# A three-block fp32 network on one core: the softmax weights in one VectorE pass, the convolution's taps earlier, and the order of work around them

## What is computed

```python
mx = silu_c @ w_ada[i] + b_ada[i]              # shifts and scales, 6 x 1024 per stream
hx = modulate(rmsnorm(x, norm1_g[i]), sx1, ax1)
px = hx @ w_in[i]                              # conv input (2 x 512), q, k, v, gates
...
z = a * sigmoid(g)                             # then 31-tap depthwise conv over tokens,
...                                            # LayerNorm over 512 channels, silu
q_x = apply_rope(rmsnorm(q_x, q_norm_g[i]), cos, sin)   # rms per head part of 64
...
p = jax.nn.softmax(s, axis=-1)                 # two maps per head
w = p[:, :, 0] - lam * p[:, :, 1]
out = einsum('bhqk,bkhv->bqhv', w, vals)       # per head RMSNorm after it
```

## Time and profile before

| | |
|---|---|
| median of 3 runs | 2174.09 us |
| profiled execution, its own time | 2172.95 us |
| its span in the profile | 2171.2 us |
| TensorE matmul busy | 2041.7 us (94%), 13834 instructions |
| VectorE busy | 1403.8 us (65%), 2190 |
| ScalarE busy | 977.3 us (45%), 1590 |
| GpSimd busy | 161.0 us (7%) |
| chain that ended last, by engine | PE 76%, DVE 16%, ACT 5%, DMA 2%, issue 1% |
| largest share of VectorE in that chain | `zc` L2068, 6% |
| one unit of 4 key blocks with its `w_ada` chunk, layer 1's attention | 3.88 us |
| a v or k chunk (96 products of 256 columns) on TensorE | 11.15 us |
| out projection of the recurrent block | 1938.1 to 1969.2 us, of it 5.95 idle |
| two of its four chunks without a wait between them | 11.46 us |
| gate columns before it end, table load before gelu ends | 1927.6, 1930.5 us |

### The profile page before, as it was taken

One profiled execution on the slowest core, in us unless ns is written; L12 is line 12 of the kernel. 1 busy time (PEld: TensorE's weight loads), 2 busy tenths in 40 slices (PEclk: granted clock), 3 DMA queues, 4 the chain that ended last, 5 costly groups with the idle time before them and its releaser, 6 DMA issues.

```text
span 2171.2 us, 35612 instructions
## 1 busy us (share of the span) xinstructions
PE 2041.7 (94%) x13834; PEld 1797.3 (83%) x13834; DVE 1403.8 (65%) x2190; ACT 977.3 (45%) x1590; POOL 161.0 (7%) x174
## 2 busy tenths in 40 slices
PE   5998799999899999989989989999999999979998
PEld 4898666888688888879967989999898998878997
DVE  5499798534455555578967667776756455775554
ACT  3334276323523232365356464445824444574442
POOL 0000000000010000000000003223120111000110
PEclk8999999999999999999999999999999999999999
DMA  7222166222122222224246545554202555443553
GB/s 295 98 78 78 59 239 228 97 97 95 61 97 97 97 97 97 97 98 137 78 154 217 186 144 185 183 193 173 104 21 78 177 190 193 158 154 118 191 180 110
DMA packets 40891, 294.51 MB, mean 136 GB/s; under 512 B 4544, under 2 KB 4544, under 8 KB 5456
## 3 DMA queue, kind: packets, MB, share of 16 engines
q1 hardware_dynamic: 40464, 290.73, 37.4%
q0 software_dynamic: 320, 2.26, 0.3%
HBM read 291.93 MB, written 1.05 MB: 135 GB/s over the span
## 4 chain that ended last, share of the span: by engine, by line
PE 76%; DVE 16%; ACT 5%; DMA 2%; issue 1%; POOL 0%; SPq 0%; ACTq 0%; DVEq 0%; POOLq 0%
PE psum L624 17%; PE psum L626 17%; PE psum L625 17%; DVE zc L2068 6%; PE psum L936 3%; PE psum L940 3%; PE psum L937 3%; DVE weights_lo L1845 3%; PE psum L1144 2%; PE psum L744 2%; PE psum L825 2%; PE psum L664 1%; PE psum L847 1%; ACT weights_hi L1281 1%; DMA raw_weights<-in_weights 1%; PE psum L665 1%
## 5 line engine op out<-in xcount | busy, mean ns | idle before, releaser
L1845 DVE TENSOR_TENSOR weights_lo<-raw_weights,weights_hi 128x2048 fp32r<-128x2048 f32 x225 | 512.5, 2290 | 173.1 <-ACT weights_hi L1281 172.7
L1281 ACT ACTIVATE weights_hi<-raw_weights 128x2048 fp32r<-128x2048 f32 x225 | 428.3, 1908 | 156.0 <-DMA raw_weights<-in_weights 149.4
L1916 DVE SCALAR_TENSOR_TENSOR xT<-psum,mods,xT 128x256 f32<-128x256 f32 x408 | 181.0, 479 | 199.5 <-PE psum L626 196.1
L624 PE MATMUL psum<-h_hi,weights_hi 128*128 128x512 f32 (+1 forms) x832 | 280.9, 338 | 0.3 <-ACT ff L1371 0.3
L626 PE MATMUL psum<-h_lo,weights_hi 128*128 128x512 f32 (+1 forms) x832 | 279.2, 336 | 0.0
L625 PE MATMUL psum<-h_hi,weights_lo 128*128 128x512 f32 (+1 forms) x832 | 277.7, 334 | 0.0
L2676 POOL TENSOR_TENSOR ffsq<-ff 128x256 f32<-128x256 f32 (+1 forms) x128 | 118.6, 928 | 1645.4 <-ACT ff L1371 1144.4
L624 PE MATMUL psum<-weights_hi,h_hi 128*128 128x256 f32 x704 | 199.5, 283 | 6.0 <-ACT val L1459 3.2
L625 PE MATMUL psum<-weights_lo,h_hi 128*128 128x256 f32 x704 | 196.5, 279 | 0.0
L626 PE MATMUL psum<-weights_hi,h_lo 128*128 128x256 f32 x704 | 196.3, 279 | 0.0
L624 PE MATMUL psum<-g_hi,weights_hi 128*128 128x256 f32 x688 | 193.5, 281 | 0.0
(11 more groups left out here) (415 smaller groups left out, 4262.2 us busy)
## 6 DMA issues: line engine op xcount, KB each, us to landing
raw_weights<-in_weights SPq DMA_DIRECT2D x273, 1024.0 KB, 4.8
staged_x<-in_x_rows SPq DMA_DIRECT2D x1, 2048.0 KB, 10.3
masks<-in_masks POOLq DMA_DIRECT2D x1, 1152.0 KB, 6.5
ln_rows<-in_ln_rows POOLq DMA_DIRECT2D x1, 1024.0 KB, 7.2
out<-outrow SPq DMA_DIRECT2D x4, 256.0 KB, 2.0
rows<-in_rows SPq DMA_DIRECT2D x1, 584.0 KB, 10.2
consts<-in_consts SPq DMA_DIRECT2D x1, 386.0 KB, 3.3
cols<-in_cols SPq DMA_DIRECT2D x1, 306.0 KB, 2.8
```

What stands on the lines that cost most here:

```text
L624: mm(out, *pair(wh, vh), start=i == 0, stop=False)
L1281: f(w_hi[:, s, :], raw[:, s, :], ACT.Copy).then_inc(hi_done, 1)
L1845: tt_(w_lo[:, s, :], raw[:, s, :], w_hi[:, s, :].bitcast(F32), ALU.subtract).then_inc(lo_done, 1)
L1916: last = stt(xT[:, m, c], b[:, c], mods[:, l, which + m, v:v + 1], xT[:, m, c], ALU.mult, ALU.add)
```

## The change

Despite its few words it touches many places:

1. **Softmax weights.** Both sums are inverted into `small[0:16]`; one factor s0·lam/s1 is made; a single pass gives w0 + factor·w1; 1/s0 is applied to the 128 x 128 value product in `save`. A pass over 128 x 512 (L2158) goes.
2. **Conv.** The gate chunk comes before the value chunk, VectorE multiplies value and gate straight from PSUM (no copies L2046), and 24 of the 124 conv steps run before the conv input is complete, on the tiles that are. `TAPS` now counts single steps.
3. **q and k.** ScalarE squares in pieces of 64 columns with `accum_out`, which gives the sums; VectorE's reduction (L2100) goes. The v chunks go to the "d" banks.
4. **LayerNorm of the conv.** Its sum is taken in the middle of the last v chunk, the squares' sum between the first scores; inversion of the root (in pieces of 128), scaling and silu are spread into the attention loop (silu at unit 21 in layer 0, unit 10 in layer 1). The `w_ada` rows get a buffer `ada_row`.
5. **Prologue.** The `w_ada` chunks come in the order 0, 4, 1, 5, ...; shift and scale are set pair by pair; a `w_in` chunk is loaded before the last `w_ada` chunk, and `rows` after chunk 9; ScalarE does all of the scaling.
6. **Hybrid block.** `conv_rest(8)` is split: one tap before `cy_normed(0)`, two after `kb` and `ktail`; ScalarE's `keep_z(1)` comes before `conv_silu(8)`.
7. **Recurrent block.** Gate chunk 0 is copied by VectorE, chunks 2 and 3 stay in banks 4 to 7 until gelu reads them there, scans and gating go in pairs, the out projection is taken chunk by chunk (only the last one closes the sums).

The core of the diff:

```diff
-TAPS = [[3, 3, 3, 3, 2, 2, 2, 2, 4, 4, 3], [1, 1, 1, 1, 3, 3, 3, 3, 4, 4, 7]]
+TAPS = [[14, 10, 9, 9, 9, 9, 7, 7, 7, 7, 12, 12, 12], [6, 6, 1, 1, 1, 1, 10, 10, 10, 10, 22, 23, 23]]
...
+ADA_ORDER = [0, 4, 1, 5, 2, 6, 3, 7]
...
+            for c in ADA_ORDER[:-1]:
+                cols("w_ada", l, c * CC, 1)
+            cols("w_in", l, CONV_W, 1)
+            cols("w_ada", l, ADA_ORDER[-1] * CC, 1)
...
-                gemm_M(a_bank, hH, hL, 4)
-                gemm_M(a_bank, hH, hL, 4)
-                column_sums(lambda k: zc[:, k, 0:TX], CT, TX, psum[:, 6, :], "zc_ready")
-                gemm_M(a_bank, hH, hL, 4, lambda: column_sums(
-                    lambda k: zsq[:, k, 0:TX], CT, TX, psum[:, 7, :], "zsq_ready"))
+                gemm_M(d_bank, hH, hL, 4)
+                gemm_M(d_bank, hH, hL, 4)
+                gemm_M(d_bank, hH, hL, 4, lambda: column_sums(
+                    lambda k: zc[:, k, 0:TX], CT, TX, psum[:, 6, :], "zc_ready"))
...
+                moved_a()
+                z_square_sum(0)
+                moved_d()
                 scores(0)
+                for k in range(1, CT):
+                    z_square_sum(k)
                 scores(1)
-                moved_a()
-                pe.wait_ge(z_normed, t.next("z_normed", CT))
...
-            for c in range(3):
-                gemm_T(d_bank, gH, gL, T)
+            gemm_T(d_bank, gH, gL, T)
+            gemm_T(a_bank, gH, gL, T)
+            last_gates = iter((6, 7))
+            gemm_T(lambda: psum[:, next(last_gates), :], gH, gL, T)
             moved_d()
...
-            for k0 in (0, 2):
+            for k0 in (0, 2, 4):
                 acc_chunks(xcH, xcL, [k0], ready="o_split")
-            acc_chunks(xcH, xcL, [4, 6], final=True, ready="o_split")
+            acc_chunks(xcH, xcL, [6], final=True, ready="o_split")
...
+                        for g in range(CC // QK):
+                            r = slice(QK * g, QK * g + QK)
+                            last = f(qsq[:, tt, r], qs[:, c % 2, tt, r], ACT.Square,
+                                     accum_out=small[:, 4 * tt + g:4 * tt + g + 1])
+                    last.then_inc(qk_squared, t.one("qk_squared"))
...
-                    dve.wait_ge(qk_squared, t.next("qk_squared"))
-                    dve.tensor_reduce(small[:, 0:4 * n], qsq[:, 0:n, :].rearrange("p t (g d) -> p (t g) d", d=QK),
-                                             AX.X, ALU.add).then_inc(qk_ssq, t.one("qk_ssq"))
...
-                    recip(small[:, b:b + 2])
-                    tt_(small[:, b + 1:b + 2], small[:, b + 1:b + 2], lam[:, 0:1], ALU.mult).then_inc(dve_step, t.one("dve_step"))
+                    dve.reciprocal(small[:, r:r + 2], small[:, b:b + 2]).then_inc(dve_step, t.one("dve_step"))
                     dve.wait_ge(dve_step, t.at("dve_step"))
-                    ts(w0, w0, small[:, b:b + 1], None, ALU.mult).then_inc(dve_step, t.one("dve_step"))
+                    stt(small[:, share:share + 1], small[:, b:b + 1], lam[:, 0:1], small[:, r + 1:r + 2],
+                        ALU.mult, ALU.mult).then_inc(dve_step, t.one("dve_step"))
                     dve.wait_ge(dve_step, t.at("dve_step"))
-                    stt(w0, w1, small[:, b + 1:b + 2], w0, ALU.mult, ALU.add).then_inc(w_ready, t.one("w_ready"))
+                    stt(w0, w1, small[:, share:share + 1], w0, ALU.mult, ALU.add).then_inc(w_ready, t.one("w_ready"))
...
-                    dve.tensor_copy(qT[:, h, q * P:q * P + P], psum[:, 6 + u % 2, 0:VD]).then_inc(o_saved, t.one("o_saved"))
+                    r = 2 * (u % 8)
+                    ts(qT[:, h, q * P:q * P + P], psum[:, 6 + u % 2, 0:VD], small[:, r:r + 1], None,
+                       ALU.mult).then_inc(o_saved, t.one("o_saved"))
```

More of the change, by code:

```diff
@@ L1282, in next_hi, with chunk @@
                 t.up("chunk")
-            def chunk(tiles, evac=None):
-                next_hi()
+            def chunk(tiles, evac=None, since=0):
+                next_hi(since)
                 t.last = tiles
@@ L1443, in _ @@
                     t.last = n
+                    if c:
+                        act.wait_ge(qk_root, t.at("qk_root"))
                     for tt in range(n):
@@ L1452, in _ @@
                         turned_qk(c - 1)
-                    act.wait_ge(qk_ssq, t.next("qk_ssq"))
-                    f(small[:, 16:16 + 4 * n], small[:, 0:4 * n], ACT.Sqrt, bias=eps6, scale=1.0 / QK).then_inc(qk_root, t.one("qk_root"))
                 for c in range(4):
-                    def keep(tt, b):
+                    next_hi()
+                    t.last = 4
+                    for tt in range(4):
                         if c == 3 and tt == 2:
-                            root_of(psum[:, 7, :], TX, CONV_W, eps6)
-                        f(val[:, tt, c * CC:c * CC + CC], b[:, 0:CC], ACT.Copy).then_inc(a_free, 1)
@@ L1778, in _ @@
             next_hi()
-            for m in range(2):
-                f(gg[:, m, :], landed(), ACT.Copy).then_inc(gg_in, t.one("gg_in"))
-                act.wait_ge(gg_in, t.at("gg_in"))
-                act.sem_inc(d_free, 1)
+            t.up("g", 2)
+            t.up("d", 2)
+            act.wait_ge(d_free, t.at("d"))
             def sig(i, g, bias, done):
@@ L1797, in _ @@
             t.last = KT
-            t.n["gg_in"] = 0
             next_hi()
```

364 lines of the change are left out of this document (226 added, 138 removed).

## The result

| | before | after |
|---|---|---|
| median, us | 2175.03 (2173.4 to 2179.53, 4 runs) | 2116.00 (2111.47 to 2121.64, 4 runs) |
| after / before | | 0.9727, interval 0.9698 to 0.9756 |
| profiled execution, us | 2172.95 | 2117.66 |
| its span, us | 2171.2 | 2115.8 |

A forecast was written before the change was run, and what follows sets the result against it. TensorE, busy 94% of the span, was taken as the bound, so gains come only where it idles or runs at lower clock. Terms summed to -45.1 us: 2172.95 to 2127.9, median 1.1 higher, so 2129; range 2113 to 2146.

The forecast's parts named there:

- The recurrent block: Recurrent block: out projection starts and ends earlier, -12.9, with 2.2 taken back for LayerNorm: -10.7 us, bounds -5 and -14.5.
- The hybrid block: Hybrid block: TensorE's 4.9 us wait for `cy_normed` shrinks to under 1.5: -3.5 us, bounds 0 and -4.9.
- The softmax edit: Attention: one VectorE pass per unit goes, costed at nothing; it only makes room for the LayerNorm pieces.
- ScalarE can carry the squares: q and k chunks: squares at 0.36 us each give ScalarE 10.8 us per chunk, under TensorE's 12.2.
- Into the attention: Start of attention: squares' sum moved, unit 2 earlier, silu waiting: -1.4 us in layer 0, -1.7 in layer 1.
- The forecast by that figure of the Trainium skill: Attention, both layers: table switches at 2.66 us each, load plus drain, would cost 11 us more, 2140 instead of 2129.
- the terms for slower work and for new waits in q/k/v: q/k/v: clock gains of 3.6 us in layer 0, 0.3 in layer 1; new waits of 1.5 and 2.4 left.
- at most 0.04 x 169.6 = 6.8: q/k/v of layer 0: upper limit, in us, on the gain from the lower clock, of which 3.6 was taken.
- all handovers better: Rival: every idle us in q/k/v, hybrid and recurrent blocks gone and silu hidden, 2115 us; chance 0.10.
- The waits of rows 2 should go: q/k/v of layer 0: with VectorE relieved, TensorE's 17.1 us idle disappears; stage term -19, bounds -13 to -20.7.
- The prologue: Before layer 0's first product: earlier `w_in` chunk lets it start at about 39.7 instead of 44.2: -4.5 us.
- added small steps: Prologue: if VectorE's pairs and four `h_lo` come between differently, the gain is 0 to -6.5 us.

The follow-up runs named there:

- e6: Changed kernel with only the recurrent block put back as it was: 2126.8 us, 10.9 over the changed kernel.
- e12: Kernel before with only the softmax edit added: 2170.71 us against 2170.49 beside it, ratio 0.9992.
- e8: Changed kernel with each of the 224 squares with a sum issued twice: 2136.4 us, 20.5 over the changed kernel.
- e5: Changed kernel without early conv steps, sums on VectorE, v chunks in ScalarE's two banks: 2146.4 us, 8.0 over the same with the four banks kept.

## Why the prediction was right, and where it was short

**Right by its own steps.** The recurrent block (forecast 10.7, profile 11.1, e6 10.9): from the end of the gate columns to the end of the out projection it was 41.6 us and is 29.2, 12.4 less where 12.9 were forecast, and the LayerNorm behind it costs 2.3 more where 2.2 were. The hybrid block (3.5; 4.2; the wait went from 4.9 to 1.8, where under 1.5 was the sign). The softmax edit as nothing (e12). That ScalarE can carry the squares, and that this was the place where it could have gone the other way (e8: with the price doubled 20 us go). Into the attention: exponentials of units 0 to 2 were forecast to end 5.0, 8.6 and 13.2 us after the last v tile and ended 5.0, 8.9 and 13.4 after it, silu holds TensorE for 2.1 where 2.7 were forecast. For the table switch the row decides against the 2.66 us: exponential, load, root, load, exponential follow one another at 0.01 to 0.02 us. The forecast by that figure of the Trainium skill ("ScalarE: Activation LUTs", What ACT_TABLE_LOAD costs), 11 us more, did not come.

**Short: the terms for slower work and for new waits in q/k/v.** I took 3.6 us of clock in layer 0 out of "at most 0.04 x 169.6 = 6.8", and 0.3 in layer 1. The bound was right: the low stretches of this stage are 13.6 us at half clock, 6.8, of which 4.6 fell on work and the rest on waits. The 3.6 had no row behind it; the three stretches behind the long waits would have given 4.6. In all the slower work was 7.7, as products at 0.118 us came on top, which no row of the prediction shows, and 2.7 in layer 1 (there -10.8 in all, of which 6.4 idle and 1.7 moved out; one low stretch behind the wait of 2.4 makes 1.7 of it). And I left 1.5 and 2.4 us of new waits (the middle sum, the q chunks of layer 1) of which one of 0.4 came: the squares are 0.24 us and not 0.36, so the root is early, and VectorE uses its slack over the whole stage. 4.1 + 1.5 in layer 0, 2.4 + 2.4 in layer 1: 10.4, which is what the forecast lacked. Both stages left their bounds: without the sums moved out -24.8 where -13 to -20.7 were given, and -9.1 where -1 to -6.8 were. The bounds in layer 0 left out what the prediction itself allowed the clock, 6.8 instead of 3.6.

**Beside a rival, by chance.** The median of 2116.0 is 1 us from the rival "all handovers better", 2115, and 13 from the forecast. Of that rival's five terms two came, the idle time of q/k/v in both layers (4.1 of 13.8 us). Silu still holds TensorE for 2.1 us in layer 0, the hybrid block keeps a wait of 1.8, and the recurrent block gained 0.4 more than forecast, not 3.8. The rest is the slower work above and 3 to 4 us by which the medians of the two kernels lie further apart than their profiled executions.

**Wrong in its reason.** "The waits of rows 2 should go" as VectorE is relieved is half of it. The exchange of banks for v has no term in the prediction, and e5 prices it at 8 us where VectorE is still late. With VectorE relieved, its part can be smaller; the kernel after with v in two banks was not run, so what the exchange is worth by itself stays open.

**The prologue** gave 3.5 of 4.5. ScalarE began hi at 34.37, where 34.2 was forecast, but VectorE was then at a pair of `h_lo` (35.93 to 37.14), so lo ran from 37.14 to 39.4 instead of ending at 38.4, and the last row's save stood behind it: the "added small steps" that the prediction gave as its bound. No experiment isolates this one, and the missing 1.0 us is within what executions differ by: twelve of them with this prologue start the first product between 38.8 and 41.0.

**Unchanged stretches:** 1.9 us were lost between the attention of layer 1 and the hybrid block, 1.2 gained before the recurrent block. Nothing was changed there, and the granted clock differs between the two executions: by one less the clock, 6.8 against 5.1 us are lost in the first stretch and 3.7 against 5.1 in the second, 1.7 and 1.4 us of difference. That is scatter and not the change's.

## What to carry to other kernels

When an engine off the bound is late in one stage, sum its work over the stage against the bound's, not chunk by chunk: the waits show up where it is asked for something, and taking away one cause or another brings nearly the same until both are back. Price a wait of TensorE from the stretch behind it as well as from its own length; here that was 1.5 to 3.0 us more behind most waits of 2.1 to 8.6 us, so many middling waits can be dearer than one long one. Before calling a difference of a stage the edit's, look at the same stage in other executions of the same code. An edit that frees an engine off the bound can be worth nothing alone (e12) and may be what makes the next one possible: test it at both ends, added to the old kernel and taken from the new.
